# Hybrid decoder step on one core: in six of eight tiles, half of the expert pairs come as one 8 KB piece instead of two 4 KB rows

## The reference

```python
val, idx = lax.top_k(s, PEER_TOPK)
...
sv, si = lax.top_k(cand, PEER_TOPK)
eidx = jnp.take_along_axis(cidx, si, axis=-1)
g = jax.nn.softmax(sv, axis=-1)
ue = jnp.take(peer_u, eidx, axis=0)
act = jax.nn.gelu(jnp.einsum('thkd,td->thk', ue.astype(f32), xk.astype(f32)), approximate=False)
ve = jnp.take(peer_v, eidx, axis=0)
return jnp.einsum('thk,thkd->td', g * act, ve.astype(f32)).astype(h.dtype)
```

## Time and profile before

| | |
|---|---|
| median of 3 runs | 3768.2 us |
| the profiled execution | 3731.76 us, span 3730.0 us |
| PE busy | 2881.6 us (77%) |
| DVE busy | 2804.2 us (75%) |
| POOL busy | 2234.3 us (60%) |
| ACT busy | 735.9 us (20%) |
| moved by DMA | 1294.61 MB, mean 347 GB/s |
| queue of POOL's gathers | 1082.25 MB, 74.2% of the 16 engines' span |

### The profile page before, as it was taken

How to read it: one execution, slowest core, us unless ns; L and a number is a source line. 1 busy time by engine, 2 the same in 40 slices (tenths; PEclk the granted TensorE clock), 3 DMA queues, 4 the chain that set the end, 5 groups by cost and what they waited for, 6 DMA issues and landing times.

```text
span 3730.0 us, 33134 instructions
## 1 busy us (share of the span) xinstructions
PE 2881.6 (77%) x10016; PEld 1798.5 (48%) x10016; DVE 2804.2 (75%) x5740; ACT 735.9 (20%) x1784; POOL 2234.3 (60%) x1820
## 2 busy tenths in 40 slices
PE   8888589788687999788988776978769755655665
PEld 6777566456562666453665344635556311111111
DVE  0641797887788957876879997888788867777776
ACT  1321113322111123223111111422211111111111
POOL 0000076787567656875766777778767776555553
PEclk9899799999898998888999888989879877777677
DMA  4124399999999999989999999999999998999997
GB/s 153 46 87 167 116 405 403 360 358 401 421 391 357 384 354 333 337 318 371 389 396 389 326 389 372 394 353 361 387 421 398 330 392 366 426 426 426 426 426 329
DMA packets 304256, 1294.61 MB, mean 347 GB/s; under 512 B 35288, under 2 KB 44528, under 8 KB 251184
## 3 DMA queue, kind: packets, MB, share of 16 engines
q0 software_dynamic: 260352, 1082.25, 74.2%
q1 hardware_dynamic: 43728, 210.25, 14.5%
HBM read 1276.77 MB, written 17.66 MB: 347 GB/s over the span
## 4 chain that ended last, share of the span: by engine, by line
DMA 26%; PE 23%; POOL 21%; DVE 16%; issue 9%; DVEq 2%; ACT 1%; PEld 1%; PEldq 0%; ACTq 0%; SPq 0%; POOLq 0%
POOL ringb L662 20%; DMA ringb<-in_v,eidx 9%; PE bank L926 8%; DMA ringb<-in_uv,eidx 7%; PE vsum L836 6%; DVE ringb L1428 4%; PE bank L1123 3%; DMA arena<-in_uv,eidx 3%; DMA n2t<-in_uv,eidx 2%; DVE acc L1473 2%; DMA wring<-in_uv,eidx 2%; PE bank L966 2%; DVE scT L1844 1%; DMA ringb<-in_u,eidx 1%; PE bank L982 1%
## 5 line engine op out<-in xcount | busy, mean ns | idle before, releaser
L662 POOL DMA_INDIRECT ringb<-in_u,eidx x768 | 920.3, 1198 | 859.5 <-DVE eidx L1539 455.3
L836 PE MATMUL vsum<-ringb,diag 128*128 128x512 f32 x1908 | 1081.8, 711 | 416.9 <-DMA ringb<-in_v,eidx 261.2
L662 POOL DMA_INDIRECT ringb<-in_v,eidx x768 | 921.6, 1200 | 327.0 <-issue 219.9
L1428 DVE CUSTOM_DVE_ANT_0 ringb<-ringb,n2t 128x1024 f32<-128x1024 f32 x776 | 922.7, 1223 | 118.0 <-DMA ringb<-in_u,eidx 56.2
L836 PEld LDWEIGHTS vsum<-ringb,diag 128*128 128x128 f32 x1908 | 399.8, 223 | 982.3 <-issue 706.1
L926 PE MATMUL bank<-wring,nTb 128*128 128x256 f32 x3024 | 686.7, 388 | 32.6 <-DMA wring<-in_w 29.0
L926 PEld LDWEIGHTS bank<-wring,nTb 128*128 128x128 f32 x3024 | 548.2, 183 | 175.0 <-DMA wring<-in_w 34.4
L1473 DVE SCALAR_TENSOR_TENSOR acc<-ringb,wgt,acc 128x1024 f32<-128x1024 f32 x354 | 454.9, 1285 | 111.7 <-DMA ringb<-in_v,eidx 107.8
L1160 ACT ACTIVATE diag<-cst,wgt 128x128 f32<-128x128 f32 x542 | 209.7, 398 | 962.4 <-DVE wgt L1445 599.3
L966 PE MATMUL bank<-nTb,wring 128*128 128x256 f32 (+1 forms) x1152 | 266.8, 390 | 6.1 <-DMA wring<-in_w 3.1
L657 POOL DMA_INDIRECT ringb<-in_uv,eidx x126 | 178.0, 1412 | 140.7 <-DVE vgb L1473 71.2
(11 more groups left out here) (290 smaller groups left out, 3080.1 us busy)
## 6 DMA issues: line engine op xcount, KB each, us to landing
wring<-in_w SPq DMA_DIRECT2D x152, 1024.0 KB, 7.8
ringb<-in_u,eidx POOLq DMA_INDIRECT x768, 7.3
ringb<-in_v,eidx POOLq DMA_INDIRECT x768, 7.5
n2t<-scratch_n SPq DMA_DIRECT2D x14, 512.0 KB, 7.1
oab<-in_xp SPq DMA_DIRECT2D x4, 1024.0 KB, 6.8
bTb<-in_keysT SPq DMA_DIRECT2D x4, 1024.0 KB, 11.4
vgb<-in_xp SPq DMA_DIRECT2D x4, 1024.0 KB, 8.9
arena<-in_s SPq DMA_DIRECT2D x8, 512.0 KB, 10.2
```

The source lines that it names most:

```text
L662: pool.indirect_dma_start(out=ring[r], out_offset=None, in_=a["u"] if kind == "u" else a["v"], in_offset=place)\
L836: last = mm(out[:, g * 512:(g + 1) * 512], lhs, row[:, g * 512:(g + 1) * 512], start=(x == first), stop=(x == end))
L1428: v.tensor_tensor_reduce(out=row, in0=row, in1=n2, scale=1.0, scalar=0.0, op0=ALU.mult, op1=ALU.add, accum_out=dg[:, m % 2, at:at + 1]).th ...
```

## The change

In the first six tiles the two pairs of a quad are no longer treated alike (`whole(x)`): the even pair stays as it was, a row of U and, 12 quads on, a row of V. The odd pair comes as one gather of 8 KB of `uv`, and its V half is summed 2 quads after its dot (`SHORT`). So:

- POOL issues per quad one U, one `uv` and one V, three gathers instead of four, of the same bytes together. The ring of 12 rows becomes 5 cells of 4 KB for the single rows and 6 slots of 8 KB (17 rows' space). The space comes from other buffers: masks are kept in bf16, constants are shortened, `gfb` is gone (the final gain is loaded into a buffer of `n2t` for each tile), squares go to buffers in use, routing results of three tiles are kept instead of four.
- Gelu of an odd pair is an instruction of its own in the quad of its dot, its weight a multiplication of one column one quad later (`agp`, `wgp`). The even pairs have groups of 8, also every eighth quad.
- The sums of a quad are an even pair's V of 12 quads before and an odd pair's of 2 quads before. PE takes the first of these first. At a tile's end PE starts on the next tile's rows only two quads after the last one was done.
- In the last two tiles the pieces are 13, five of them outside the ring (not `n2t`).

What is left out of the diff below: moved buffers, names, the waits of the new semaphores, the loads.

```diff
-RING = 12
+
+CELLS = 5
+SLOTS = 6
 LAG = 12
 SHORT = 2
-PIECES = 12
-GROUP = 16
+GROUP = 8
...
+def whole(x):
+
+    return x >= XW or (x % 2 == 1 and SEGS[ITEMS[x][0]] != "S")
+
+
+
 DRAIN = LAG // 2
 STEPS = QU + DRAIN + SHORT
 QUADS = STEPS + TAIL
 DOT_STEP = [a if a < QW else a + DRAIN for a in range(QU)]
-SUM_STEP = [a + DRAIN + SHORT if a >= QW else a + LAG if a + LAG < QW else QW + (a + LAG - QW) // 2 for a in range(QU)]
 DOTS = {DOT_STEP[a]: a for a in range(QU)}
-SUMS = {q: [a for a in range(QU) if SUM_STEP[a] == q] for q in range(QUADS + 1)}
+
+
+def sum_step(x):
+    a = x // 2
+    if whole(x):
+        return DOT_STEP[a] + SHORT
+    return a + LAG if a + LAG < QW else QW + (a + LAG - QW) // 2
+
+
+SUM_STEP = [sum_step(x) for x in range(len(ITEMS))]
+
+SUMS = {q: [] for q in range(QUADS + 1)}
+for x in sorted(range(len(ITEMS)), key=lambda x: (whole(x), x)):
+    SUMS[SUM_STEP[x]].append(x)
 SEG_STEP = [DOT_STEP[a] for a in SEG_QUAD]
-SEG_SUMS = [SUM_STEP[a] for a in SEG_QUAD]
-SEG_DONE = [SUM_STEP[a + n // 2 - 1] + 1 for a, n in zip(SEG_QUAD, SEG_ITEMS)]
-
-
-SEG_GSIZE = [2 if i >= WHOLE else GROUP for i in range(len(SEGS))]
-SEG_GROUP = [sum((n + g - 1) // g for n, g in zip(SEG_ITEMS[:i], SEG_GSIZE)) for i in range(len(SEGS))]
-GROUP_STEP = {SEG_GROUP[i] + k // SEG_GSIZE[i]: (DOT_STEP[x // 2], x) for x, (i, k) in enumerate(ITEMS)}
+SEG_SUMS = [min(SUM_STEP[x] for x, (j, _) in enumerate(ITEMS) if j == i) for i in range(len(SEGS))]
+SEG_DONE = [max(SUM_STEP[x] for x, (j, _) in enumerate(ITEMS) if j == i) + 1 for i in range(len(SEGS))]
+
+
+def groups(pick, size):
+
+    out = []
+    for i in range(len(SEGS)):
+        xs = [x for x, (j, _) in enumerate(ITEMS) if j == i and pick(x)]
+        n = size(i)
+        out += [xs[k:k + n] for k in range(0, len(xs), n)]
+    return out
+
+
+ALONE = groups(lambda x: not whole(x), lambda i: GROUP)
+PIECED = groups(whole, lambda i: 2 if i >= WHOLE else 1)
+GROUP_OF = {x: (m, xs.index(x)) for family in (ALONE, PIECED) for m, xs in enumerate(family) for x in xs}
...
-    places, n = {}, 0
+    places, n = {}, [0, 0]
     for q in range(QW + DRAIN):
-        rows = [("u", 2 * q + j) for j in range(2)] if q < QW else []
-        rows += [("v", 2 * at + j) for at in SUMS[q] if at < QW for j in range(2)]
-        for x in rows:
-            places[x] = (n % RING, n // RING)
-            n += 1
+        for x in ([("u", 2 * q), ("u", 2 * q + 1)] if q < QW else []) + [("v", x) for x in SUMS[q] if x < XW and not whole(x)]:
+            big = whole(x[1])
+            places[x] = (n[big] % (SLOTS if big else CELLS), n[big] // (SLOTS if big else CELLS))
+            if big:
+                places[("v", x[1])] = places[x]
+            n[big] += 1
     return places, n
...
+SLOT_USES = [(ROWS[1] - r + SLOTS - 1) // SLOTS for r in range(SLOTS)]
+
+LEFT = 5
+PIECES = LEFT + SLOTS + CELLS // 2
...
+    for done in SEG_DONE:
+        rate[done - 1] = 0.0
...
-    return SEGS[ITEMS[x][0]] == "S" or x % 2 < PE_ROWS[SUM_STEP[x // 2]]
-
-
-
-PE_ENDS = [(lambda xs: (xs[0], xs[-1]))([x for x, (j, _) in enumerate(ITEMS) if j == i and by_pe(x)]) for i in range(len(SEGS))]
-DVE_ROWS = [[x for x, (j, _) in enumerate(ITEMS) if j == i and not by_pe(x)] for i in range(len(SEGS))]
+    i, q = ITEMS[x][0], SUM_STEP[x]
+    if SEGS[i] == "S":
+        return True
+    return SUMS[q].index(x) < PE_ROWS[q] and (i == 0 or q >= SEG_DONE[i - 1] + 2)
+
+
+
+IN_ORDER = [x for q in range(QUADS) for x in SUMS[q]]
+PE_ENDS = [(lambda xs: (xs[0], xs[-1]))([x for x in IN_ORDER if ITEMS[x][0] == i and by_pe(x)]) for i in range(len(SEGS))]
+DVE_ROWS = [[x for q in range(QUADS) for x in reversed(SUMS[q]) if ITEMS[x][0] == i and not by_pe(x)] for i in range(len(SEGS))]
+DVE_ORDER = [x for q in range(QUADS) for x in reversed(SUMS[q]) if not by_pe(x)]
...
-            whole = q in DOTS and DOTS[q] >= QW
             rows = [("u", 2 * DOTS[q] + j) for j in range(2)] if q in DOTS else []
-            rows += [("v", 2 * at + j) for at in SUMS[q] if at < QW for j in range(2)]
+            rows += [("v", x) for x in SUMS[q] if not whole(x)]
...
                 r, n = PLACE[(kind, x)]
+                if whole(x):
+                    if n:
+                        pool.wait_ge(slot_used[r], 2 * n)
+                    pool.indirect_dma_start(out=slot[r], out_offset=None, in_=a["uv"], in_offset=place).then_inc(slot_here[r], 16)
+                    continue
                 if n:
-                    pool.wait_ge(slot_used[r], n)
-                pool.indirect_dma_start(out=ring[r], out_offset=None, in_=a["u"] if kind == "u" else a["v"], in_offset=place)\
-                    .then_inc(gathered[r], 16)
+                    pool.wait_ge(cell_used[r], n)
+                pool.indirect_dma_start(out=cell[r], out_offset=None, in_=a["u"] if kind == "u" else a["v"], in_offset=place)\
+                    .then_inc(cell_here[r], 16)
...
+                if i < WHOLE - 1 and GAIN_AT[i] == q:
+                    row_used(sp, ("u", XW - 1 if i == WHOLE - 2 else 2 * SEG_QUAD[i] + PAIRS - 1))
+                    sp.dma_start(n2t[:, gain_of(i)[1], :], a["gf"].partition_broadcast(P)).then_inc(d_gf, 16)
...
             A = nc.scalar.activation
-            for m, (at, x) in GROUP_STEP.items():
-                if at + 1 == q:
-                    i, k = ITEMS[x]
-                    width = k % SEG_GSIZE[i] + 1
-                    row_used(act, ("u", x))
-                    A(ag[:, m % 2, 0:width], dg[:, m % 2, 0:width], ACT.Gelu).then_inc(gelu_done, 1)
-            for x in [2 * at + j for at in SUMS[q + 1] for j in range(2)]:
+            if q in DOTS and 2 * DOTS[q] + 1 in GROUP_OF and whole(2 * DOTS[q] + 1):
+                x = 2 * DOTS[q] + 1
+                m, at = GROUP_OF[x]
+                row_used(act, ("u", x))
+                A(agp[:, m % 4, 0:at + 1], dgp[:, m % 4, 0:at + 1], ACT.Gelu).then_inc(gelu_pieced, 1)
+            for m, xs in enumerate(ALONE):
+                if DOT_STEP[xs[-1] // 2] + 1 == q:
+                    row_used(act, ("u", xs[-1]))
+                    A(ag[:, m % 2, :], dg[:, m % 2, :], ACT.Gelu).then_inc(gelu_alone, 1)
+            for x in SUMS[q + 1]:
                 if x not in diag_number:
                     continue
-                i, k = ITEMS[x]
-                n, m, at = diag_number[x], group_of(i, k), k % SEG_GSIZE[i]
-                act.wait_ge(wgt_ready, m + 1)
+                n = diag_number[x]
+                weight_here(act, x)
                 if n >= DIAGS:
                     row_used(act, ("v", diagonals[n - DIAGS]))
-                A(diag[:, n % DIAGS, :], ident, ACT.Copy, scale=wgt[:, m % 2, at:at + 1]).then_inc(diag_ready, 1)
+                A(diag[:, n % DIAGS, :], ident, ACT.Copy, scale=weight_of(x)).then_inc(diag_ready, 1)
...
-            for m, (at, x) in GROUP_STEP.items():
-                i, k = ITEMS[x]
-                if at + (1 if i >= WHOLE else 2) == q:
-                    dve.wait_ge(gelu_done, m + 1)
-                    if SEGS[i] == "S":
-                        TT(wzS[:, 0::NS + 1], ag[:, m % 2, 0:NS], gT[:, :], ALU.mult).then_inc(wgt_ready, 1)
-                    else:
-                        (c, t), size = tile_at(SEGS[i]), SEG_GSIZE[i]
-                        lo = k - size + 1
-                        old = [n for n, y in enumerate(diagonals) if group_of(*ITEMS[y]) <= m - 2]
-                        if old:
-                            dve.wait_ge(diag_ready, old[-1] + 1)
-                        old = [y for ys in DVE_ROWS for y in ys if group_of(*ITEMS[y]) <= m - 2]
-                        if old:
-                            row_used(dve, ("v", old[-1]))
-                        TT(wgt[:, m % 2, 0:size], ag[:, m % 2, 0:size], gate[:, c % 2, t, lo:lo + size], ALU.mult).then_inc(wgt_ready, 1)
+                                       accum_out=dgp[:, m % 4, at:at + 1] if whole(x) else dg[:, m % 2, at:at + 1]).then_inc(used(("u", x))[0], 1)
+
+            def weights(family, m, xs, into, out, gelu, ready, depth):
+
+                i, k = ITEMS[xs[0]]
+                dve.wait_ge(gelu, m + 1)
+                if SEGS[i] == "S":
+                    TT(wzS[:, 0::NS + 1], out[:, m % depth, 0:NS], gT[:, :], ALU.mult).then_inc(ready, 1)
+                    return
+                before = [y for ys in family[:max(0, m - depth + 1)] for y in ys]
+                old = [diag_number[y] for y in before if y in diag_number]
+                if old:
+                    dve.wait_ge(diag_ready, max(old) + 1)
+                old = [y for y in DVE_ORDER if y in before]
+                if old:
+                    row_used(dve, ("v", old[-1]))
+                step = xs[1] - xs[0] if len(xs) > 1 else 1
+                TT(into[:, m % depth, 0:len(xs)], out[:, m % depth, 0:len(xs)],
+                   gate[:, slot_of(*tile_at(SEGS[i])), k:k + step * (len(xs) - 1) + 1:step], ALU.mult).then_inc(ready, 1)
+
+            for m, xs in enumerate(PIECED):
```

(12 more changed lines are left out.)

214 lines of the change are left out of this document (120 added, 94 removed).

## The result

| | median | runs |
|---|---|---|
| before | 3770.3 us | 3760.4 to 3775.8 (4 runs) |
| changed | 3834.8 us | 3829.0 to 3836.4 (4 runs) |

The ratio is 1.0171, with a 95% interval of 1.0147 to 1.0196. The forecast was 3739 us, the range ended at 3812.

What follows compares the result with a forecast made beforehand. POOL was taken to bound nine stretches of the first six tiles, DMA the last two tiles. Terms -65 - 8 + 12 + 22 + 10 + 0 = -29 us on 3731.8 gave 3702.8, in the runs' terms 3739 us; range 3655 to 3812.

Steps and rivals of the forecast that it cites:

- A shorter ring: Single rows reuse a cell after 2.5 quads instead of 3, so POOL waits longer: +10 us (0 to +50).
- POOL's relief: Fewer gathers free POOL in nine 100 us stretches, until near DVE's bound: -65 us (-122 to 0).
- ACT: Added gelus and 74 more table loads on ACT, with DVE waiting for gelu in each quad: +22 us (0 to +95).
- the nine stretches: Nine stretches of 100 us in the first six tiles, where POOL was taken as 97.5% occupied and everybody waits for it.
- What is late next?: After POOL in the nine stretches: DMA's ceiling would allow -122 us, DVE's -68; the lower gain was taken.
- DMA packets: Half of the bytes in packets twice as long, on seven DMA-bound stretches: -8 us (-15 to 0).
- DVE outside the stretches: 46 us of added DVE work outside the nine stretches, a quarter of it on the path: +12 us (0 to +46).
- The two ends: More bytes in the first 12 quads, fewer at tile six's end, sample-row waits there: taken as equal, 0 (-20 to +25).
- Rival 3: ACT stands in each quad until DVE's second dot, so PE waits for diagonals: 3800 us, chance 0.24.
- rival 4: Memory already at its limit, some 364 GB/s, so a shorter POOL only queues transfers: 3805 us, chance 0.02.
- Rivals 1 and 2: First: whole gain down to DMA's ceiling, 3681 us, chance 0.17. Second: DVE keeps half its idle time, 3765 us, 0.17.

Runs made afterwards that it cites:

- two neighbours in form: Seven cells and five slots with the odd pair's weight multiplied twice, 3761.2 us, or with that weight ahead of the next dots, 3759.9 us.

## Why the prediction was wrong

**The step that failed is "A shorter ring", +10 us with an upper end of 50.** It measured +58.5 in the old form, and seven cells for five took 79 us off the new one. With it fell "POOL's relief", -65, which measured nothing at this room. With +58 for the ring, 0 for the relief and for ACT, and -8 and +12 kept as they stood, the sum is 62 us; measured were 64.4, and 61.5 on one chip. How close that comes is partly luck, since the two kept terms were never measured. Three things were wrong. The first is the scaling: POOL's 292 us of waits times 3 / 2.5 (58 us more, not "some 50"; its fifth is 12). In the new form they became 976 us, because a POOL with one gather fewer in each quad arrives at each cell earlier and waits there instead of issuing. Most of these some 680 us more fill time that POOL no longer needs (606 us), so no fixed share of them is paid: the loss is 9% of them. The second is the share: I took a fifth of the added waits, POOL's share of the chain, as paid. In the ten-place ring, where POOL's work is unchanged, 58 of 72 to 82 us were. A share of the chain is an average over what happened before; it doesn't say what an added wait costs at an engine whose lateness everyone downstream inherits. The third is that the slots "look further ahead" by less than their number says, since a piece stays two quads longer; with six slots this did no harm, with five and four it did.

**POOL's relief** was right in its direct sign (1783 us busy in all, 384 gathers fewer, its waits put down to DVE and PE; forecast about 1850, since an 8 KB gather beside the rows took 1156 ns and not the 1412 of the last tiles) and wrong in what it gives here: where over 380 GB/s and DVE at 90% were forecast, the nine stretches now show 309 to 359 GB/s and DVE at 70 to 91%, 80.5% on average. "What is late next?" had two candidates, DMA's ceiling and DVE's. The missing one was the room itself: how far ahead POOL may issue, in quads, of each kind of place. At equal room, 2.5 quads, the old form (1.0146) and the new (1.0162, on another chip) can't be told apart; the relief is worth nothing there. With seven cells, five slots and the gelu last, the new form gains 51 us. That this is near the −65 − 8 + 12 of the sum shows no more than the size: in the nine stretches that kernel has 368 GB/s and DVE at 86.3% on average, still short of the forecast's signs.

**DMA packets, DVE outside the stretches**: small, and never seen apart. Doubling DVE's weight work cost nothing with seven cells, so +12 was probably high. **ACT**: forecast +22 with up to +95; the 198 table loads came, and at five cells they cost nothing. DVE waited 12.0 us for the gelu in all; 74 loads less moved nothing. ACT did cost time, but by the place of its gelu and with more room: 34 us. By the Trainium skill (ScalarE: Activation LUTs, What ACT_TABLE_LOAD costs), a switch to another table also drains the engine for about 1380 ns and takes 2.66 us in all. The trace of the changed kernel disagrees: where ACT has its next work ready, a switch takes 1.30 us at best, and 1.32 us in these lines, from the end of one instruction to the start of the next.

```profile
1573.61 0.21 ACT L1390 ACTIVATE tS<-tS 128x32 f32<-128x32 f32 x1
1573.84 1.28 ACT L1392 ACT_TABLE_LOAD   x1
1575.14 0.23 ACT L1392 ACTIVATE aS<-yS 128x32 f32<-128x32 f32 x1
```

**The two ends**: the last tiles kept their 426 GB/s, and the loss lies ahead of them. The wait at the sample rows came, and the stretch 3100 to 3200 us is at 273 GB/s, but only in part as described: the sixth to eighth sample row wait 5.7 us for PE, and the fourth 13.9 us for DVE's `acc`, the sum of an earlier row. What this stretch by itself costs was not measured; the term of 0 for the two ends stays open, as far as it isn't in the 58 us.

**Rival 3, lockstep.** Its sign in the profile came: PE's waits for diagonals rose from 46.5 to 189.2 us for weight loads alone, above the 100 set for it, and its price of 3800 us was, beside rival 4's 3805, the nearest to 3834.8. It was still not the cause. Taking the wait away gave nothing until the cells were there, and then 34 us. Without that experiment its waits would have passed for the reason. **Rival 4** (memory at 358 to 368 GB/s): the average of 363 GB/s looks like it. The Trainium skill (DMA: Bandwidth & Descriptors, Specifications) names limits of about 358 and 368 GB/s; the trace disagrees, since the same work with seven cells and the gelu last runs at 377 GB/s and the last tiles at 426. **Rivals 1 and 2** fall with the forecast: they need DVE at 85% or more in the nine stretches, and it was at 80.5%.

## What to carry over

Count the room of a ring in steps of the consumer, for each kind of place apart, before and after, and from the gather to the last use that frees the place: if one queue issues into several kinds, the shortest room paces all of them, and it deserves a rival of its own when it shrinks, however many bytes the rest gained. When an issuing engine is relieved, the first thing that can be late next is its own room, so ask what the relief turns into there, and don't price the wait as a small share of a chain. A wait that grows in the profile is a suspect, not a cause: take it away, and see whether the time moves or only the wait's name.

## What the runs showed of the hardware

Chips of one kind differed by 1.3% on one kernel, in medians of ten to fifteen runs (3731.5 against 3777.5, 3778.7 and 3779.2 us), with dots of 1223 ns in each profile and matmuls of 697 to 711 ns. That holds for one kernel and not for another: seven cells and their two neighbours in form lie within 5 us of each other on the same chips. So a ratio to another kernel carries that kernel's chip with it, and two forms are best compared on one chip. Table loads took 1283 ns each everywhere, and 74 of them cost no time where ScalarE was 23% busy. A switch of table took 1.30 us at best, and under 1.4 us in 121 of the 197 in the changed kernel's trace that have an instruction on both sides; no further drain shows. A gather of an 8 KB piece occupied POOL for 0.94 us at best, as one of a 4 KB row did, with 0.30 us ahead of either.
